# Two-layer hybrid decoder trunk: the down product moved behind the next expert's gate/up product, and part of the fourth expert's weights fetched ahead

## What is computed

```python
def hier_moe(x, w_group, w_router, w_gate, w_up, w_down):
    # top-1 of 4 groups, then top-2 of its 8 experts: 32 experts in all
    ...
    # for the rows of each expert
    h = silu(rows @ w_gate[e]) * (rows @ w_up[e])      # 1024 -> 512
    y = h @ w_down[e]                                   # 512 -> 1024
    # weighted sum of the two experts of each token
    ...
```

## Time and profile before

| | |
|---|---|
| Median of 3 runs | 1636.38 us (1635.76 to 1638.82) |
| Profiled execution: its own time | 1636.7 us |
| Its span from the first to the last instruction | 1634.6 us |
| Mean granted share of TensorE's clock | 0.995 |
| TensorE busy | 1577.5 us (97%) |
| DVE / ACT / POOL busy | 484.7 / 360.8 / 197.6 us |
| Bytes moved, mean | 474.21 MB, 290 GB/s |
| Expert loop of layer 0, of layer 1 (starts of the first gate/up product, end of the last down product) | 326.56 to 787.48 us, 1155.69 to 1617.47 us |

### The profile page before, as it was taken

How to read it: one execution, slowest core, us unless ns; L and a number is a source line. 1 busy time by engine, 2 the same in 40 slices (tenths; PEclk the granted TensorE clock), 3 DMA queues, 4 the chain that set the end, 5 groups by cost and what they waited for, 6 DMA issues and landing times.

```text
span 1634.6 us, 21323 instructions
## 1 busy us (share of the span) xinstructions
PE 1577.5 (97%) x8068; PEld 738.3 (45%) x8072; DVE 484.7 (30%) x1252; ACT 360.8 (22%) x853; POOL 197.6 (12%) x298
## 2 busy tenths in 40 slices
PE   7999989999999999999799999999999999999995
PEld 4545664543333333333445468855433333333332
DVE  1485851531111111111514125734511111111114
ACT  2354461311111111111200246732111111111110
POOL 2240320000000000000102022420000000000000
PEclk9999999999999999999999999999999999999999
DMA  8620127389999999999933320052899999999997
GB/s 244 258 103 7 54 55 308 124 345 420 423 421 421 422 422 422 422 422 419 353 50 104 142 56 1 2 235 78 345 421 421 421 422 421 422 421 422 422 422 310
DMA packets 118314, 474.21 MB, mean 290 GB/s; under 512 B 40822, under 2 KB 47222, under 8 KB 68333
## 3 DMA queue, kind: packets, MB, share of 16 engines
q1 hardware_dynamic: 110156, 456.98, 69.8%
q10 hardware_dynamic: 3136, 8.40, 1.3%
q0 software_dynamic: 4960, 8.04, 1.3%
HBM read 454.84 MB, written 26.77 MB: 295 GB/s over the span
## 4 chain that ended last, share of the span: by engine, by line
PE 67%; SPq 12%; DMA 4%; DVE 3%; issue 1%; ACT 1%; POOL 0%; DVEq 0%; POOLq 0%
PE bank L1951 19%; SPq L1897 10%; PE bank L1964 9%; PE bank L1543 8%; PE bank L1924 8%; PE bank L597 7%; DMA arena<-in_moe_w_up 3%; PE bank L409 3%; PE bank L444 3%; PE bank L1939 2%; SPq L1906 2%; PE bank L426 2%; PE bank L1957 1%; DVE arena L2476 1%; PE bank L458 1%
## 5 line engine op out<-in xcount | busy, mean ns | idle before, releaser
L1951 PE MATMUL bank<-arena 128*64 128x512 f32 x2048 | 451.4, 592 | 6.3 <-DMA arena<-in_moe_w_up 5.9
L1951 PEld LDWEIGHTS bank<-arena 128*64 128x64 f32 x2048 | 143.6, 137 | 302.1 <-issue 291.0
L1964 PE MATMUL bank<-arena 128*64 128x512 f32 x1024 | 230.6, 592 | 2.1 <-DVE arena L2057 2.1
L2053 DVE TENSOR_TENSOR arena<-arena,bank 128x256 f32<-128x256 f32 x64 | 27.0, 422 | 637.2 <-ACT arena L2043 637.1
L1970 POOL DMA_INDIRECT y_d<-arena,slot_row x62 | 60.7, 979 | 857.9 <-ACT arena L2048 830.7
L1924 PE MATMUL bank<-arena 128*64 128x512 bf16 x1272 | 160.1, 381 | 0.2
L1543 PE MATMUL bank<-arena 128*128 128x512 f32 x320 | 139.1, 593 | 0.8 <-ACT arena L321 0.8
L1964 PEld LDWEIGHTS bank<-arena 128*64 128x64 f32 x1024 | 71.9, 137 | 124.1 <-issue 110.5
L2043 ACT ACTIVATE arena<-bank 128x256 f32<-128x256 f32 x64 | 24.6, 384 | 410.5 <-PE bank L1951 410.5
L597 PE MATMUL bank<-arena 128*128 128x512 f32 x256 | 111.8, 594 | 0.0
L895 PE MATMUL bank<-arena 128*128 128x512 f32 (+1 forms) x288 | 105.3, 525 | 0.0
(11 more groups left out here) (319 smaller groups left out, 1505.0 us busy)
## 6 DMA issues: line engine op xcount, KB each, us to landing
arena<-in_moe_w_gate SPq DMA_DIRECT2D x128, 1024.0 KB, 20.2
arena<-in_moe_w_up SPq DMA_DIRECT2D x128, 1024.0 KB, 23.0
arena<-in_moe_w_down SPq DMA_DIRECT2D x62, 2048.0 KB, 23.3
arena<-in_even_w_in SPq DMA_DIRECT2D x4, 2048.0 KB, 8.4
y_d<-arena ACTq DMA_DIRECT2D x2, 4096.0 KB, 16.8
arena<-y_d SPq DMA_DIRECT2D x8, 1024.0 KB, 9.3
arena<-bias_row_d SPq DMA_DIRECT2D x2, 3584.0 KB, 11.9
arena<-in_odd_w_in SPq DMA_DIRECT2D x3, 2048.0 KB, 14.2
```

Of the source, the lines that this page charges most:

```text
L1951: mm = nc.tensor.matmul(bank[1][fh * CAP:(fh + 1) * CAP, :], xeT[:, j, half * CAP:(half + 1) * CAP], wgu[u][:, :, n, fh * FH:(fh + 1) * FH ...
L1964: mm = nc.tensor.matmul(bank[3][dh * CAP:(dh + 1) * CAP, :], hidT[:, j, fh * CAP:(fh + 1) * CAP], wd[u][:, n, dh * 512:(dh + 1) * 512], st ...
```

## The change

Five things change, all in the mixture of experts and in the program's set-up.

- TensorE's order: down(c-1) now stands right behind gate_up(c) instead of at the end of expert c-1. Behind it come x_turn(c+1), hid_turn(c), and all of the picking for c+2 in one piece. The last experts: in the body of expert 30 both down(29), behind gate_up(30), and down(30), behind hid_turn(30), stand ahead of gate_up(31); in the body of expert 31 down(31) stands behind hid_turn(31).
- ACT's order follows: `y_out(c-1)` stands behind `silu(c)`, ahead of `rows_out(c+2)`.
- SP's order: the down weights of expert c+2 are now issued in `next_weights(c)`, behind both halves of expert c+3's gate/up, once `dn` of c-1 is there. Expert 31's down weights come last.
- A new on-chip buffer `early` of 12 KB a partition takes 3 of the first 4 row blocks of gate and of up of expert 3 (1.5 MiB in two DMAs), fetched ahead of the loop. When `guh` of expert 0 comes, only the fourth row block is still to be fetched (0.5 MiB), to `wgu[0]`. gate_up(3) reads the first three blocks from `early`; for that the body of expert 3 is written out by hand on TensorE.

```diff
+EARLY = 3
...
+        early = sb("early", [P, 2, EARLY, FF])
...
+        def some_rows(sp, dst, layer, e, n, a, b):
+            h = a // 4
+            src = ins[("moe_w_gate", "moe_w_up")[n]][layer, bass.ds(e, 1), h * 512:(h + 1) * 512].rearrange("e (p j) f -> p e j f", j=4)
+            return sp.dma_start(dst.rearrange("p (e j) f -> p e j f", e=1), src[:, :, a - 4 * h:b - 4 * h])
...
-        def gate_up_mms(u, h):
+        def gate_up_mms(u, h, begun=0):
             for n in range(4 * h, 4 * h + 4):
                 half, j = n // 4, n % 4
+                w = early if n < begun else wgu[u]
...
-        def pick_begin(pe, t, c):
+        def picked(pe, t, c):
             pe.wait_ge(S(f"{t}_ones"), c + 1)
             pe.wait_ge(S(f"{t}_rows"), c + 1)
-            pick_rows(range(2))
...
+            pick_rows().then_inc(S(f"{t}_picked"), 1)
...
+            for n in range(2):
+                some_rows(sp, early[:, n], L, RING, n, 0, EARLY).then_inc(S("m_early"), 16)
 
             def next_weights(c, u):
                 sp.wait_ge(S(f"{t}_guh"), c + 1 + L * NE)
-                half_weights(sp, t, L, c + RING, u, 0)
+                if isinstance(c, int) and c == 0:
+                    for n in range(2):
+                        some_rows(sp, wgu[u][:, n, EARLY:4], L, RING, n, EARLY, 4).then_inc(S(f"{t}_wgu{u}"), 16)
+                else:
+                    half_weights(sp, t, L, c + RING, u, 0)
                 sp.wait_ge(S(f"{t}_gu"), c + 1 + L * NE)
                 half_weights(sp, t, L, c + RING, u, 1)
                 if u == 0 and isinstance(c, int) and c == 0:
...
+                else:
+                    next_down(c - 1, (u - 1) % RING)
+
+            def next_down(c, u):
                 sp.wait_ge(S(f"{t}_dn"), c + 2 + L * NE)
                 down_weights(sp, t, L, c + RING, u)
...
+            next_down(NE - RING - 1, (NE - RING - 1) % RING)
...
             def body(e, c, cu, u, after):
-                gate_up(pe, t, c, cu, u)
-                if isinstance(c, int) and c == L * NE:
+                opening = isinstance(c, int) and c == L * NE
+                refilled = isinstance(c, int) and c == L * NE + RING
+                if refilled:
+                    pe.wait_ge(S("m_early"), past("m_early") + 32 * (L + 1))
+                gate_up(pe, t, c, cu, u, EARLY if refilled else 0)
+                if not opening and after >= 1:
+                    down(pe, t, c - 1, cu - (u == 0) + L * (uses((u - 1) % RING) - uses(u)), (u - 1) % RING)
+                if opening:
...
                 if after >= 1:
                     x_turn(pe, t, c + 1)
-                if after >= 2:
-                    pick_begin(pe, t, c + 2)
                 hid_turn(pe, t, c)
                 if after >= 2:
-                    pick_end(pe, t, c + 2)
+                    picked(pe, t, c + 2)
+                else:
+                    down(pe, t, c, cu, u)
...
-                down(pe, t, c, cu, u)
...
-            per_expert(pe, L, body)
+            per_expert(pe, L, body, alone=1)
...
                 silu(act, t, c)
                 if isinstance(c, int) and c == L * NE:
                     rows_out(act, t, c + 1)
+                elif after >= 1:
...
+                    y_out(act, t, c - 1, (u - 1) % RING)
                 if after >= 2:
                     rows_out(act, t, c + 2)
-                if isinstance(c, int) and c == L * NE:
-                    act.wait_ge(S(f"{t}_routed"), past("m_routed") + L + 1)
-                y_out(act, t, c, u)
+                else:
+                    y_out(act, t, c, u)
...
-    nc = bacc.Bacc("TRN2", target_bir_lowering=False, num_devices=1)
+    nc = bacc.Bacc("TRN2", target_bir_lowering=False, num_devices=1, dynamic_dma_scratch_size=4096)
```

More of the change, by code:

```diff
@@ L161 @@
     "m_lones": ("y_gated", 4), "mx0_yin": ("brow", 2), "mx1_yin": ("relb_ones", 1),
-    "m_cnt": ("ix_mm", 12), "m_routed": ("selm", 3),
+    "m_early": ("ix_relu", 12), "m_cnt": ("ix_mm", 12), "m_routed": ("selm", 3),
 }
@@ L1892, in build @@
         x_row_f, x_no_row = at(EW + 1024, 1), at(EW + 1025, 1)
+        def some_rows(sp, dst, layer, e, n, a, b):
+            h = a // 4
+            src = ins[("moe_w_gate", "moe_w_up")[n]][layer, bass.ds(e, 1), h * 512:(h + 1) * 512].rearrange("e (p j) f -> p e j f", j=4)
+            return sp.dma_start(dst.rearrange("p (e j) f -> p e j f", e=1), src[:, :, a - 4 * h:b - 4 * h])
         def one_half(sp, t, layer, e, u, n, h):
-            src = ins[("moe_w_gate", "moe_w_up")[n]][layer, bass.ds(e, 1), h * 512:(h + 1) * 512].rearrange("e (p j) f -> p e (j f)", j=4)
-            sp.dma_start(wgu[u][:, n, 4 * h:4 * h + 4].rearrange("p (e j) f -> p e (j f)", e=1), src).then_inc(S(f"{t}_{('wgu', 'wgv')[h]}{u}"), 16)
+            some_rows(sp, wgu[u][:, n, 4 * h:4 * h + 4], layer, e, n, 4 * h, 4 * h + 4).then_inc(S(f"{t}_{('wgu', 'wgv')[h]}{u}"), 16)
         def half_weights(sp, t, layer, e, u, h):
@@ L1945, in gain_x @@
                                            ALU.mult)
-        def gate_up_mms(u, h):
+        def gate_up_mms(u, h, begun=0):
             for n in range(4 * h, 4 * h + 4):
                 half, j = n // 4, n % 4
+                w = early if n < begun else wgu[u]
                 for fh in range(2):
                     mm = nc.tensor.matmul(bank[1][fh * CAP:(fh + 1) * CAP, :], xeT[:, j, half * CAP:(half + 1) * CAP],
-                                          wgu[u][:, :, n, fh * FH:(fh + 1) * FH], start=(n == 0), stop=(n == KD - 1))
+                                          w[:, :, n, fh * FH:(fh + 1) * FH], start=(n == 0), stop=(n == KD - 1))
             return mm
@@ L2014, in x_turn, with gate_up @@
             turn_rows().then_inc(S(f"{t}_xturn"), 1)
-        def gate_up(pe, t, c, cu, u):
+        def gate_up(pe, t, c, cu, u, begun=0):
             pe.wait_ge(S(f"{t}_xT"), c + 2)
@@ L2019, in gate_up @@
             pe.wait_ge(S(f"{t}_wgu{u}"), 32 * (cu + 1))
-            gate_up_mms(u, 0).then_inc(S(f"{t}_guh"), 1)
+            gate_up_mms(u, 0, begun).then_inc(S(f"{t}_guh"), 1)
             pe.wait_ge(S(f"{t}_wgv{u}"), 32 * (cu + 1))
@@ L2057, in hid_out, with per_expert @@
             nc.vector.tensor_copy(hidT, split(bank[2][:, 0:2 * P], 2, P)).then_inc(S(f"{t}_hT"), 1)
-        def per_expert(eng, L, body, first=None):
+        def per_expert(eng, L, body, first=None, alone=0):
             def one(e, cu, u, after):
                 body(e, e + L * NE, cu + L * uses(u), u, after)
-            for u in range(RING):
-                one(u, 0, u, 2)
-                if u == 0 and first:
+            for e in range(RING + alone):
+                one(e, e // RING, e % RING, 2)
+                if e == 0 and first:
                     first()
[L2067 to L2071, removed]
+            ends = TRIPS - (alone > 0)
+            with eng.Fori(1, ends) as it:
+                for k in range(alone, alone + RING):
+                    one(it * RING + k, it + k // RING, k % RING, 2)
+            for e in range(RING * ends + alone, NE):
+                one(e, e // RING, e % RING, min(2, NE - 1 - e))
         def uses(u):
@@ L2295, in body @@
                     rows_out(act, t, c + 1)
+                elif after >= 1:
+                    if isinstance(c, int) and c == L * NE + 1:
+                        act.wait_ge(S(f"{t}_routed"), past("m_routed") + L + 1)
+                    y_out(act, t, c - 1, (u - 1) % RING)
                 if after >= 2:
                     rows_out(act, t, c + 2)
-                if isinstance(c, int) and c == L * NE:
-                    act.wait_ge(S(f"{t}_routed"), past("m_routed") + L + 1)
-                y_out(act, t, c, u)
+                else:
+                    y_out(act, t, c, u)
                 if after == 1:
```

## The result

The changed kernel takes 1651.88 us (median of 4 runs, 1649.77 to 1654.24), the kernel before 1637.48 us beside it (4 runs, 1635.76 to 1638.82): a ratio of 1.0089, 95% interval 1.007 to 1.0107. It is slower, as forecast, by 14.4 us where 19.6 were expected. The profiled execution of the changed kernel took 1652.59 us, its span is 1650.7 us (before 1634.6), its mean clock 0.989 (before 0.995). The medians, ranges and ratios of the experiments leave out two slow executions at lower mean clocks, 2837.73 us (early fetch without the new order, 0.648) and 1675.24 us (new order without the early fetch, 0.943).

A forecast was written before the change was run, and what follows sets the result against it. The weight stream, about 1 us per expert slower than TensorE, was taken as the bound. The layer's end adds 9.8 us, twice: 1636.7 + 19.6 = 1656.3, with the median 0.3 lower, 1656.0 us; range 1646 to 1661.

The forecast's parts named there:

- The first hole: Dry stretch of the weight stream at 330 to 331 us (4 GB/s); the early fetch fills it, worth 0.
- the second: Dry stretch from 344 us to the stream's restart, 3.7 us; predicted to grow by what the earlier one loses.
- The rival in which both holes close: Layer start: early fetch lets the stream end 4.7 us a layer earlier, 1646.6 us; chance 0.12.
- the faster rival: Loop: 4096 bytes of descriptor memory speed the stream to 14.7 from 15.3 us an expert, 1630.4 us; chance 0.05.
- The wait for down 30: Layer end: TensorE's down(30) waits some 11 us for weights landing 10 us later than before, gate_up(31) queued behind.
- D: Time expert 30's down weights land and TensorE's wait ends: predicted 778.1 us, in layer 1 1608.1.
- down(30) at the low clock: Layer end: after the idle stretch down(30) begins at 1.2 GHz, 3.65 + 1.5 us; bounds nothing to +3.65.
- The rival without any loss of clock: Layer end: clock doesn't fall in the wait, 1.5 us less a layer, 1653.0 us; counted inside the forecast.
- The scatter: Layer end: POOL's last scatter, ahead of the fetch of scattered rows, taken as 6.0 us, bounded by 3.8 and 6.5.
- The first fetched MiB: Layer end: first part of the scattered rows fetched back, into an idle queue, 4.8 us.
- The products' line: Layer end on TensorE: down(30), transposes, gate_up(31), to the last down's end; D + 18.5, shift +9.1 us.
- the scattered rows decide: Layer end: down(30), POOL's issue, scatter and fetch reach D + 17.5 and set the loss, +9.8 us a layer.

## Why the prediction was right, and where it was not

**The bound and the period.** That the stream, not TensorE, sets the loop holds: the period fell by 0.32 us an expert and the restored end (ratio 0.9995) shows no gain from it. The size was off: I had bounded the change of order at 0.1 us an expert, and it was 0.32, from turns and picking in one piece. TensorE uses up its lead sooner, so 16 waits of some 1.2 us appear that I had not named. They are free, as the argument wanted.

**The start.** The first hole is filled, the second is not, and the restart is at its old place. Worth 0, as predicted; the run without the new order (1.0001) confirms it for early fetch and descriptor memory together, and the run without these (1.0092) from the other side. The rival in which both holes close and the stream ends 4.7 us a layer earlier didn't happen, since the second stayed open. Nor was the second worth its 3.7 us when it was filled on purpose: the stretch from restart to end moved by 0.8 and 1.5 us, with the first hole open again.

**The stream and the ring memory.** No trace shows a faster stream, and the faster rival is out: with 4096 bytes and the early fetch the ratio is 1.0001. Of the Trainium skill's best guess ("DMA: Bandwidth & Descriptors", section Latency and other measured facts) this says only that a smaller ring together with the early fetch gives nothing here; single engines weren't looked at.

**The end of the layer.** The wait for down 30 is there, 10.70 and 10.90 us for the predicted 11, with D = 777.5 for 778.1, and gate_up(31) queued behind it. This is the cause, shown twice: by the old end put back (1.0089 to 0.9995) and by the new order alone (1.0092). From D to DVE's adds I had D + 17.5; the trace has D + 16.0. Term by term:

- down(30) at the low clock: 5.15 predicted, 5.70 and 6.46 measured. The loss of clock was mis-sized, 1.5 for 2.05 and 2.8 us, inside its bounds. The run with TensorE kept busy puts between 4 and 5 us on it in all. The rival without any loss of clock is out.
- From there to POOL's issue: 1.4, and 784.62 - 783.21 = 1.4.
- **The scatter: 6.0 predicted, 2.4 measured** (2.6 in layer 1). This is the term that failed most. I took it near its own row, 6.5 us, but that row was a scatter beside the stream, and the low bound, 3.8, was an ordinary load. In this kernel, with the stream ended, it took less than either, so my bounds didn't hold it.
- The first fetched MiB: 4.8 predicted, 5.3 measured.
- The products' line, to the end of the last down product: D + 18.5 predicted, 792.83 + 3.65 = 796.48 measured, D + 19.0.

That the number came out so near is partly luck. The scatter alone put each layer's sum about 3.6 us too high; the clock (0.6 and 1.3), the fetch (0.5) and the time from the landing to the adds (1.1 and 0.7), which I had at nothing, made good 4.7 of these 7.1 us.

**Which line decides.** The sentence that the scattered rows decide is wrong for this kernel, by little. With the short scatter they are there at D + 14.9, and DVE is not free before hid_out(31), at D + 15.3; in layer 1 the two are 0.2 us apart. I had followed gate_up(31) only through TensorE, to the end of the last down product, and had not put hid_out(31), which stands ahead of the adds on DVE, into the sum: down(30) and the transposes to D + 6.2, 7.1 us of gate/up, then silu, turn and copy, end at D + 15.3, and the adds begin at D + 16.0, behind 0.7 us (0.45 in layer 1) for which the profile shows no wait. With the lines this close, moving gate_up(31) out of the way could bring 1.1 us at most without a shorter way to the scattered rows, and there that way became longer.

The shift of the adds against D is +8.3 us in layer 0 and (1632.14 - 1615.65) - (1616.05 - 1608.15) = +8.6 in layer 1, for the predicted 9.8 twice. D came 0.6 us sooner than before in layer 0, and in layer 1 0.2 us sooner than that layer's shift alone would put it; 8.3 + 8.6 - 0.8 is the 16.1 us of the two spans.

## What to carry to other kernels

Putting a consumer one step back in this pipeline was free as long as the pipeline ran, and was paid at its end, where the last items come late and have work behind them: write the end out by hand in its old order. A gap that is closed in a stream that waits for permissions comes back for the most part at the next place where it waits for one, unless the permissions move as well. And when two lines lead to an end, follow each through every engine's own queue; an edit that cures one is worth only the distance to the next.

## What was unexpected in the hardware

- The same scatter of one expert's rows takes 6.5 to 6.8 us from issue to landing beside the weight stream, and once the stream had ended 2.4 and 2.6 us in the changed kernel, but 4.4 and 4.1 us with gate_up(31) ahead of down(30), where the stream had ended as well. Why the last are longer stays open.
- The clock fell not only in a wait of 10.7 us: with 3.3 us idle behind a stretch of short turns, gate_up(31) ran at a low clock (0.62 in the mean of 775 to 780 us) and took 9.27 us, 9.56 in layer 1, instead of 7.09. What it hangs on was not measured.
- The opening of layer 0's loop comes at times up to 4.3 us apart in the traces of these kernels (gate_up(0) at 324.60 to 328.87 us), and 4.0 us apart in two that are alike up to there (324.75 in the changed kernel, 328.72 with gate_up(31) ahead of down(30)). It shifts whole timelines, so ends of layers are compared by their distance from D, not by their times.
